# Perceptron down products of a float32 transformer kernel: seven products of block sums per eighth instead of eight block products

## The chip, the cores and the metric

The kernel runs on one NeuronCore of a Trainium2 chip. Its engines work side by side from their own instruction streams and meet at semaphores: TensorE (PE, matmul; its weight loads are shown apart as PEld), VectorE (DVE), ScalarE (ACT), GpSimd (POOL), and SyncE (SP), which issues the loads from the chip's memory. The metric is the device time of one execution, in microseconds (us). A measurement of this kernel can tell a change of about 0.2% (4 us).

## The reference, cut to what matters

The program is three transformer blocks on 512 tokens of width 1024, in float32. The first has a mixture of experts, the other two (layers l = 0 and l = 1 here) end in the perceptron that the change is about:

```
x = x + relu(rms_norm(x, mlp_norm[l]) @ w1[l]) ** 2 @ w2[l]     # x: 512 x 1024, w1: 1024 x 4096, w2: 4096 x 1024
```

After layer 0's perceptron come the projections and the attention of layer 1, after layer 1's the final norm and the output.

## The kernel before

Every engine's instructions are written out by hand in the order in which they run, and semaphores say what waits for what.

**Split products.** A float32 operand a is split as a = hi + lo, where hi is a rounded to the narrower type fp32r and lo = a - hi. A product is three matmuls, hi*hi, hi*lo, lo*hi, added up in a PSUM bank (`split_product`, recorded at L1311). ACT makes each hi (a Copy into an fp32r tile), and a subtraction makes each lo: POOL for weights (`w_lo`, L1023), DVE for activations. Each matmul has 128 rows of contraction and a 128 x 512 result.

**The perceptron.** The 4096 hidden features are done in eighths of 512, in the order up0, up1, down0, up2, down1, ... up7, down6, down7 (`MLP_STEPS`). An up step is four jobs of 24 matmuls (8 blocks of contraction x 3), one for each 128 features; ACT takes the result out of PSUM with Relu and squares it into `hid_hi`, DVE squares it too and subtracts for `hid_lo`. A down step is eight jobs of 12 matmuls (4 blocks x 3): four token tiles t for the first 512 columns of the result, four for the second; DVE adds each job's result to x (`add_to_x`, 128 x 512). So an eighth is 96 + 96 = 192 matmuls.

**PSUM.** Of the eight banks the jobs of the perceptron use two in turn, `psA0` and `psA1`: a job may begin when the result of the job two before it is taken out (semaphores `proj_ready`, `proj_evacuated`). The pairs `psS`, `psT` and `psO` belong to the attentions and are idle in the perceptrons.

**Weights.** Each step's 2 MB of weights comes by one DMA into one of three slots of `ring`. ACT and POOL split them in two halves of 128 x 2048 per step into two pairs of buffers; a half can be split when the half two before it is used up (`then_split`). The last step of layer 0 and both output projections ("ao", "no") end in a norm that is woven in (`norm`, `tail`): per tile of 128 tokens an addition to x, the mean square on ACT and DVE, transposes on PE, and a split of the turned result, whose lo part POOL makes for tiles 0 and 1 and DVE for tiles 2 and 3 (`hT_lo`). The first up job of a layer (`first_hidden`, L1420) takes the first three token tiles in its 384-column matmuls and the fourth in 128-column ones.

Of the kernel before, what the change touches and what calls it, by code (L numbers as in the profile page):

```python
# [6 lines left out]
F32 = mybir.dt.float32  # L7
# [6 lines left out]
P = 128  # L14
# [93 lines left out]
EIGHTHS = 8  # L108
UP_JOBS, DOWN_JOBS = NF // EIGHTHS, 2 * NT

# [13 lines left out]
MLP_JOBS = EIGHTHS * (UP_JOBS + DOWN_JOBS)  # L124

# [60 lines left out]
def split_pieces():  # L186
# [23 lines left out]
    for l, name in enumerate(("ao", "no")):  # L210
# [3 lines left out]
        for kind, e, first in MLP_STEPS:  # L214
            if kind == "up":
                stage(f"up{l}{e}", KD, halves, f"mlp{l}", first, 2)
            else:
                stage(f"down{l}{e}", UP_JOBS, ((0, 512), (512, 1024)), f"mlp{l}", first, NT)
# [10 lines left out]
for _n, _piece in enumerate(SPLIT):  # L229
    SPLIT_AT.setdefault(_piece[0], _n)  # L230
MERGE_AT = {_piece: SPLIT_AT["cp"] + _n for _n, _piece in enumerate(MERGE_ORDER)}
# [94 lines left out]
def build(nc, w, out):  # L326
    ctx = ExitStack()
    with ctx:
# [93 lines left out]
        w_lo = [over(f"w_lo{i}", [P, 2048], "big", 8192 + 2048 * i) for i in range(2)]  # L422
        last_hi, last_lo = [w_lo[0], w_hi[1]], [w_lo[1], w_hi[0]]
        hid_hi = [over(f"hid_hi{i}", [P, UP_JOBS, T], *at) for i, at in enumerate((("tok", 0), ("big", 12288)))]
        hid_lo = [over(f"hid_lo{i}", [P, UP_JOBS, T], *at) for i, at in enumerate((("tok", 2048), ("big", 14336)))]
# [91 lines left out]
        squared = sem("squared")  # L517
        hidden_hi = sem("hidden_hi")
# [205 lines left out]
        S, PR = ([scr[:, i, :] for i in at] for at in ((0, 1), (2, 3, 4)))  # L724

# [87 lines left out]
        slot_of = {n: i % RING for i, n in enumerate(in_ring)}  # L813
# [4 lines left out]
        for name, pieces, _ in plan:  # L818
            if name != "experts":
                total[slot_of[name]] += 16 * len(pieces)  # L820
                arrived_at[name] = total[slot_of[name]]

# [10 lines left out]
        def last_use(name, last):  # L833

            if last == "ax":
                return ax_ready, NT
            if isinstance(last, str):
# [6 lines left out]


# [16 lines left out]
        def raw_piece(c):  # L862

            name, k, c0, c1, _, _ = SPLIT[c]
            words = [pieces[0][1] for n, pieces, _ in plan if n == name][0]
            return slot(name)[:, 0:words].rearrange("p (k n) -> p k n", k=k)[:, :, c0:c1]

        def part(parts, c):

            _, k, c0, c1, _, _ = SPLIT[c]  # L870
            if c < SPLIT_AT["ao0"]:
# [18 lines left out]
        def piece_used(eng, c):  # L890

            if SPLIT_AT["cp"] <= c < SPLIT_AT["ai"]:
# [23 lines left out]
        def _(sp):  # L916
# [75 lines left out]
            for name, pieces, last in plan:  # L992
# [16 lines left out]
                held[s] = last_use(name, last)  # L1009

# [7 lines left out]
        def _(pool):  # L1018
# [82 lines left out]
            def layer(l, out):  # L1101

                split_weight(SPLIT_AT[out + "0"] + 1)
                for c in range(3):
                    then_split(SPLIT_AT[out + "0"] + c)
# [1982 lines left out]
```

## Time and profile before

| | us |
|---|---|
| median of three runs | 2098.33 |
| lowest and highest | 2096.97, 2100.91 |
| the profiled execution | 2099.13 |
| its span, from the first to the last instruction | 2097.3 |

The profiled execution is the one that all rows below come from. It is 0.8 us longer than the median; its span leaves out 1.8 us around the instructions. A row's busy time is the sum of the durations of an engine's instructions; a matmul's end is modelled, so the time from one matmul's start to the next tells its cost, not its duration. "idle before" is the time an engine stood still ahead of an instruction, with what released it.

### The profile page before, as it was taken

To read this page: it belongs to the slowest core of one execution; us is meant where nothing else is said; L and a number is where in the kernel's file an instruction comes from. 1 tells how busy PE (TensorE), PEld (TensorE's weight loads), DVE (VectorE), ACT (ScalarE), POOL (GpSimd) and SP (SyncE) were. 2 spreads that over 40 slices of the span, in tenths; PEclk is the share of its full clock that TensorE was granted. 3 is DMA by queue.
4 is the path that set the end of the run, shared out by engine and by line. 5 is a ranking of instruction groups with operands and counts; after the bars stand their busy time and mean duration, and the time that the engine had idled before them with its cause. 6 is when DMAs were issued, how large, how long until landed. Compare 5 with 4: busy or idle time off the path is not lost.

```text
span 2097.3 us, 27184 instructions
## 1 busy us (share of the span) xinstructions
PE 1911.0 (91%) x10934; PEld 1483.5 (71%) x10934; DVE 748.4 (36%) x1736; ACT 706.8 (34%) x1303; POOL 687.8 (33%) x395
## 2 busy tenths in 40 slices
PE   7999999598885999988999999999799999999998
PEld 6877778432222793457888888888667797888886
DVE  2160343511111525863322222222566623222223
ACT  5123551311111423363423222242267633222322
POOL 2343232011101220154344444443056444444342
PEclk9999999799998899999999999999899999999999
DMA  6232103689998330201223232221500022232311
GB/s 226 81 114 87 41 1 141 260 333 419 420 421 314 112 113 9 80 1 42 81 89 112 81 119 82 83 62 41 121 1 2 2 81 81 80 121 81 121 41 40
DMA packets 82319, 248.44 MB, mean 118 GB/s; under 512 B 12259, under 2 KB 15523, under 8 KB 69904
## 3 DMA queue, kind: packets, MB, share of 16 engines
q1 hardware_dynamic: 75936, 231.54, 30.0%
q0 software_dynamic: 4880, 9.89, 1.3%
q10 hardware_dynamic: 1376, 5.25, 0.6%
q8 instruction: 88, 1.44, 0.3%
q14 instruction: 39, 0.32, 0.1%
HBM read 241.89 MB, written 12.58 MB: 121 GB/s over the span
## 4 chain that ended last, share of the span: by engine, by line
PE 50%; DVE 3%; issue 2%; ACT 1%; POOL 0%; DVEq 0%; ACTq 0%
PE psA L1311 41%; PE psO L1784 2%; PE psT L1821 1%; PE psS L1812 1%; PE psA L1420 1%; PE psO L1371 1%; PE psA L1812 1%; PE psT L1403 1%; DVE scr L3041 1%; ACT big L1853 1%; PE psA L1728 0%; PE psA L1180 0%; DVE scr L2333 0%; DVE nsa_q L2333 0%; PE psO L1774 0%
## 5 line engine op out<-in xcount | busy, mean ns | idle before, releaser
L1023 POOL TENSOR_TENSOR w_lo<-ring,w_hi 128x2048 fp32r<-128x2048 f32 (+2 forms) x43 | 194.9, 4534 | 282.5 <-ACT w_hi L1853 282.5
L2333 DVE TENSOR_TENSOR x<-psA,x 128x512 f32<-128x512 f32 (+1 forms) x176 | 108.7, 618 | 324.6 <-PE psA L1311 320.6
L1853 ACT ACTIVATE w_hi<-ring 128x2048 fp32r<-128x2048 f32 (+2 forms) x65 | 117.6, 1808 | 236.6 <-PE psA L1311 236.6
L1311 PE MATMUL psA<-w_hi,hid_hi 128*128 128x512 f32 x512 | 178.7, 390 | 0.0
L1311 PE MATMUL psA<-w_lo,hid_hi 128*128 128x512 f32 x512 | 178.6, 390 | 0.0
L1311 PE MATMUL psA<-hT_hi,w_hi 128*128 128x512 f32 x504 | 176.8, 390 | 0.0
L1311 PE MATMUL psA<-hT_hi,w_lo 128*128 128x512 f32 x488 | 171.9, 390 | 0.0
L1853 ACT ACTIVATE big<-psA 128x512 f32<-128x512 f32 (+6 forms) x149 | 66.2, 468 | 279.8 <-PE psA L1311 150.1
L2333 DVE TENSOR_TENSOR scr<-scr 128x512 f32<-128x512 f32 (+2 forms) x69 | 62.2, 903 | 275.0 <-ACT hid_hi L1853 274.8
L1311 PE MATMUL psA<-w_hi,hid_lo 128*128 128x512 f32 x384 | 149.6, 390 | 0.0
L1853 ACT ACTIVATE scr<-scr,stat 128x384 f32<-128x384 f32 (+3 forms) x224 | 124.4, 556 | 71.0 <-DVE stat L3041 39.1
L1311 PE MATMUL psA<-hT_lo,w_hi 128*128 128x512 f32 x376 | 146.4, 389 | 0.0
L1023 POOL TENSOR_TENSOR ring_lo<-ring,early_hi 128x1024 fp32r<-128x1024 f32 x36 | 87.1, 2423 | 165.5 <-ACT early_hi L1853 165.5
L1023 POOL TENSOR_TENSOR w_hi<-ring,w_hi 128x2048 fp32r<-128x2048 f32 x18 | 83.2, 4620 | 111.2 <-ACT w_hi L1853 111.2
L1853 ACT ACTIVATE scr<-psA 128x512 f32<-128x512 f32 x64 | 38.2, 597 | 234.5 <-PE psA L1311 218.1
L1023 POOL TENSOR_TENSOR w_lo<-ring,w_lo 128x2048 fp32r<-128x2048 f32 x17 | 78.3, 4606 | 113.8 <-ACT w_lo L1853 113.8
L1156 POOL TENSOR_SCALAR scr<-scr,stat,big 128x128 f32<-128x128 f32 (+3 forms) x128 | 77.0, 612 | 117.2 <-DVE stat L3003 116.9
L1311 PE MATMUL psA<-w_hi,hT_hi 128*128 128x256 f32 (+2 forms) x384 | 108.9, 283 | 5.8 <-DVE tok L2337 2.7
L1311 PEld LDWEIGHTS psA<-w_hi,hid_hi 128*128 128x128 f32 x512 | 96.2, 188 | 20.2 <-DVE scr L2333 0.2
L1311 PEld LDWEIGHTS psA<-w_lo,hid_hi 128*128 128x128 f32 x512 | 96.2, 188 | 19.9
L1311 PEld LDWEIGHTS psA<-hT_hi,w_hi 128*128 128x128 f32 x504 | 94.7, 188 | 19.6
L1311 PE MATMUL psA<-w_lo,hT_hi 128*128 128x256 f32 (+2 forms) x384 | 108.3, 282 | 0.0
(358 smaller groups left out, 4528.1 us busy)
## 6 DMA issues: line engine op xcount, KB each, us to landing
ring<-in_mlp_w SPq DMA_DIRECT2D x32, 2048.0 KB, 8.4
ring<-in_w_in SPq DMA_DIRECT2D x8, 2048.0 KB, 7.9
ring<-in_w_gate_e SPq DMA_DIRECT2D x14, 1024.0 KB, 17.3
ring<-in_w_up_e SPq DMA_DIRECT2D x14, 1024.0 KB, 21.4
ring<-in_w_down_e SPq DMA_DIRECT2D x13, 1024.0 KB, 27.9
big<-in_w_down_e SPq DMA_DIRECT2D x12, 1024.0 KB, 27.5
ring<-in_ab_w_in SPq DMA_DIRECT2D x5, 2048.0 KB, 8.0
scr<-in_w_down_e SPq DMA_DIRECT2D x7, 1024.0 KB, 26.7
```

What stands on the lines that cost most here:

```text
L1023: nc.gpsimd.tensor_tensor(part(w_lo, c), raw_piece(c), part(w_hi, c).bitcast(F32), ALU.subtract)\
L1156: nc.gpsimd.tensor_scalar(at, at, fac[:, n_items + i:n_items + i + 1], gate3[:, it["t"], it["head"], 1 + it["branch"]:2 + it["branch"]], A ...
L1311: ins = pe.matmul(o, a, b, start=(at == 1), stop=(at == 3 * len(terms)))
L1371: ins = pe.matmul(o[HD * half:HD * (half + 1), t * P:(t + 1) * P], v[:, b, 2 * it["hp"] + half, :], pt[half][:, b * P:(b + 1) * P], start= ...
L1403: ins = pe.transpose(psT[k % 2][:, b * P:(b + 1) * P], pair_probs[k % PROBS][:, b * P:(b + 1) * P], ident)
L1420: ins = pe.matmul(o[:, some], a[:, k, 0:P], b[:, k, some], start=(k == 0 and a is wh and b is hT_hi), stop=(k == KD - 1 and a is wl))
L1784: ins = pe.matmul(o[HD * g:HD * (g + 1), at:at + P], v2[:, b, branch, g, 0:HD], pt[g][:, b * P:(b + 1) * P], start=(it["first"] and not br ...
L1812: ins = pe.matmul(o[:, 0:it["n"]], query(4 * it["c"] + it["j"], it["g"])[:, it["t"] * P:(it["t"] + 1) * P], nsa_k[:, it["branch"], it["g"] ...
L1821: ins = pe.transpose(psT[k % 2][:, b * P:(b + 1) * P], probs[k % PROBS][:, b * P:(b + 1) * P], ident)
L1853: return nc.scalar.activation(o, i, f, **kw)
L2333: return nc.vector.tensor_tensor(o, a, b, op)
L3041: nc.vector.tensor_tensor_reduce(out=at, in0=score_bank(i)[:, 0:it["n"]], in1=cmask(it["t"]), scale=-1.0, scalar=3e38, op0=ALU.add, op1=AL ...
```

## The change

In down0 to down6 the product of the hidden block H (512 tokens x 512 features) and the weight block W (512 features x 1024 columns) is done by Strassen's scheme in Winograd's manner. H is cut in four parts a11, a12, a21, a22 (256 tokens x 256 features), W in b11, b12, b21, b22 (256 features x 512 columns). Instead of eight products of parts there are seven, q = 0 to 6, of parts and of sums of parts, and each is added into one, two, three or four quarters of x:

| q | hidden part | weight block | goes to quarters of x | kept in |
|---|---|---|---|---|
| 0 | a12 | b21 | 1 | psA |
| 1 | a11 | b11 | 4 | psS |
| 2 | a12 less a sum | b22 | 1 | psA |
| 3 | a21 + a22 | b12 - b11 | 2 | psT |
| 4 | a11 - a21 | b22 - b12 | 2 | psA |
| 5 | a sum of three | a sum of three | 3 | psO |
| 6 | a22 | b21 less a sum | 1 | psA |

A product q is two token tiles x two blocks of contraction x three = 12 matmuls. The products 0, 2, 4, 6 ("shared") go through `psA` and DVE adds them to x in each down step, in 2, 2, 4 and 2 additions of 128 x 512. The products 1, 3 and 5 ("kept") are added up in the six banks of `psS`, `psT` and `psO` over all seven down steps, and DVE adds them to x once, in 18 additions, during down7. down7 itself stays as it was, except that its weights are split in four pieces.

The work around it changes as follows.

- ACT writes the squares as plain float32 into `raw`. DVE makes four sums of hidden parts (`sum_part`), ACT rounds seven parts (`round_part`) and DVE makes their seven lo parts (`low_part`), all 128 x 512. Two of the parts are rounded after the second up job, two after the fourth, the last three (with the sums they need) at the start of the next up step, while PE does the down step before them or that up step.
- DVE makes four sums of weight blocks in place in the ring (`sum_block`) and the seven lo parts of weight blocks (`low_block`), 128 x 1024 each. POOL no longer touches the weights of down0 to down6.
- All weight pieces of the perceptrons are 128 x 1024 and go through four slots (`w_slot`): piece i can be rounded when piece i - 4 is used up.
- The perceptrons' weights use two slots of the ring; the third holds hidden parts. The slot of a down step's weights is free when the last of its lo parts is made.

The core of the diff (the helpers of DVE and PE; ACT's `round_weight` and `round_part` are a wait and a Copy each):

```
 EIGHTHS = 8
+LAST = EIGHTHS - 1
+PRODUCTS, KEPT, SHARED = 7, (1, 3, 5), (0, 2, 4, 6)
...
+        hidden_parts = [a12, a11, spare, a21, spare, a11, a22]
+        PART_ORDER = (1, 4, 0, 6, 3, 5, 2)
...
+            def down_part(l, e, q):
+
+                pe.wait_ge(down_hi, PRODUCTS * (LAST * l + e) + q + 1)
+                pe.wait_ge(down_lo, PRODUCTS * (LAST * l + e) + q + 1)
+                wh, wl = operand(l, MLP_PIECE_AT["down", e, q])
+                hi, lo = (hid_parts[l, e % 2, q, low] for low in range(2))
+                for t in range(2):
+                    at = slice(t * P, (t + 1) * P)
+                    if q in SHARED:
+                        split_product(job(f"mlp{l}", MLP_FIRST["down", e] + 2 * SHARED.index(q) + t), 512,
+                                      [(hi[:, k, at], lo[:, k, at], wh[:, k, :], wl[:, k, :]) for k in range(2)])
+                        continue
...
+                    for k in range(2):
+                        for a, b in ((hi, wh), (hi, wl), (lo, wh)):
+                            ins = pe.matmul(KEPT_BANK[q][t][:, :], a[:, k, at], b[:, k, :],
+                                            start=(not e and k == 0 and a is hi and b is wh),
+                                            stop=(e == LAST - 1 and k == 1 and a is lo))
...
+            def sum_block(l, e, q):
+
+                n = BLOCK_SUMS.index(q)
+                b11, b12, b21, b22 = (quarter(l, e, k, j) for k in range(2) for j in range(2))
+                if n != 1:
+                    dve.wait_ge(down_lo, PRODUCTS * (LAST * l + e) + (2, None, 4, 6)[n])
...
+                o, a, b = ((b11, b12, b11), (b12, b22, b12), (b11, b22, b11), (b11, b21, b11))[n]
+                tt(o, a, b, ALU.subtract).then_inc(block_sum, 1)
...
             def mlp(l):
                 for kind, e, first in MLP_STEPS:
...
+                    if kind == "up":
+                        if e:
+                            hidden_tail(l, e - 1)
+                            low_block(l, e - 1, 0)
...
+                            low_block(l, e - 1, 1)
+                            sum_block(l, e - 1, 3)
+                            sum_block(l, e - 1, 4)
+                        if e < LAST:
+                            sum_part(l, e, 4)
+                            low_part(l, e, 0)
+                            low_part(l, e, 1)
...
+                            low_block(l, e - 1, 2)
...
+                    elif e < LAST:
+                        low_block(l, e, 3)
+                        add_shared(l, e, 0)
+                        sum_block(l, e, 5)
+                        low_block(l, e, 4)
+                        low_block(l, e, 5)
+                        add_shared(l, e, 2)
+                        sum_block(l, e, 6)
+                        low_block(l, e, 6)
+                        add_shared(l, e, 4)
+                        add_shared(l, e, 6)
```

How this moves instructions is shown at two places. First DVE in a steady down step of layer 0. Before, the hidden block's last square and lo part stand ahead of the eight additions to x, and the next up step follows:

```order
L2333 TENSOR_TENSOR scr<-scr 128x512 [waits hidden_hi]
L2333 TENSOR_TENSOR hid_lo_70<-scr,hid_hi_68 128x512 [waits squared]
L2333 TENSOR_TENSOR x<-psA,x 128x512 [waits proj_ready] x8
L2333 TENSOR_TENSOR scr<-scr 128x512 [waits hidden_hi]
L2333 TENSOR_TENSOR hid_lo_71<-scr,hid_hi_69 128x512 [waits squared]
```

Now the same engine in a down step, from the lo part of product 3's weights (the first row) to the last addition; `ring<-ring` is a sum of weight blocks, `w_slot<-ring,w_slot` the lo part of one:

```order
L2508 TENSOR_TENSOR w_slot_69<-ring,w_slot_69 128x1024 [waits down_hi]
L2508 TENSOR_TENSOR x<-psA,x 128x512 [waits proj_ready] x2
L2508 TENSOR_TENSOR ring<-ring 128x2x512 [waits block_sum,down_lo]
L2508 TENSOR_TENSOR w_slot_71<-ring,w_slot_71 128x1024 [waits down_hi]
L2508 TENSOR_TENSOR w_slot_68<-ring,w_slot_68 128x1024 [waits down_hi]
L2508 TENSOR_TENSOR x<-psA,x 128x512 [waits proj_ready] x2
L2508 TENSOR_TENSOR ring<-ring 128x2x512 [waits block_sum,down_lo]
L2508 TENSOR_TENSOR w_slot_70<-ring,w_slot_70 128x1024 [waits down_hi]
L2508 TENSOR_TENSOR x<-psA,x 128x512 [waits proj_ready]
L2508 TENSOR_TENSOR x<-psA,x 128x512
L2508 TENSOR_TENSOR x<-psA,x 128x512 [waits proj_ready]
L2508 TENSOR_TENSOR x<-psA,x 128x512
```

So the additions that free PE's banks now queue behind weight work on the same engine, and four of them take one bank twice. Second, DVE in down7 of layer 0, where before only eight additions stood: the kept sums (from `psS`, `psT`, `psO`) are put between the first four of them.

```order
L2508 TENSOR_TENSOR x_49<-psA0,x_49 128x512 [waits proj_ready,sum_taken]
L2508 TENSOR_TENSOR x_49<-psS0,x_49 128x512 [waits down_product]
L2508 TENSOR_TENSOR x_49<-psS1,x_49 128x512 [waits down_product]
L2508 TENSOR_TENSOR x_49<-psS0,x_49 128x512 [waits down_product]
L2508 TENSOR_TENSOR x_49<-psA1,x_49 128x512 [waits proj_ready,sum_taken]
L2508 TENSOR_TENSOR x_49<-psS1,x_49 128x512 [waits down_product]
```

## Rows read from the trace of the kernel before

**Rows 1.** The page: busy time of each engine; the chain that ended last.

```profile
PE 1911.0 (91%) x10934; PEld 1483.5 (71%) x10934; DVE 748.4 (36%) x1736; ACT 706.8 (34%) x1303; POOL 687.8 (33%) x395
...
PE psA L1311 41%; PE psO L1784 2%; PE psT L1821 1%; PE psS L1812 1%; PE psA L1420 1%; PE psO L1371 1%; PE psA L1812 1%; PE psT L1403 1%; DVE scr L3041 1%; ACT big L1853 1%; PE psA L1728 0%; PE psA L1180 0%; DVE scr L2333 0%; DVE nsa_q L2333 0%; PE psO L1774 0%
```

**Rows 2.** Stretches: length, busy PE, PEld, DVE, ACT, POOL, granted clock, DMA share, GB/s.

```profile
1060.00:1360.00 300.00, 300.00 (x1325) 248.56 (x1324) 83.85 (x112) 83.90 (x80) 128.99 (x28) 1.00 0.26 92
1780.00:2080.00 300.00, 300.00 (x1326) 248.53 (x1325) 83.36 (x113) 81.06 (x77) 124.39 (x27) 1.00 0.22 78
1072.10:1115.62 43.52, 43.52 (x193) 36.05 (x193) 12.01 (x17) 12.37 (x13) 18.42 (x4) 1.00 0.28 97
```

**Rows 3.** Timeline, PE: matmuls around the start of down1 (start, duration).

```profile
1112.73 0.39 PE L1311 MATMUL psA<-w_hi,hid_hi 128*128 128x512 f32 x1
...
1115.45 0.39 PE L1311 MATMUL psA<-w_hi,hid_hi 128*128 128x512 f32 x1
```

**Rows 4.** Timeline, DVE and POOL in one eighth.

```profile
1072.13 0.69 DVE L2333 TENSOR_TENSOR x<-psA,x 128x512 f32<-128x512 f32 x1
...
1108.78 1.63 DVE L2333 TENSOR_TENSOR scr<-scr 128x512 f32<-128x512 f32 x1 [4.02 <-ACT hid_hi L1853]
...
1115.65 0.69 DVE L2333 TENSOR_TENSOR x<-psA,x 128x512 f32<-128x512 f32 x1
1118.37 0.69 DVE L2333 TENSOR_TENSOR x<-psA,x 128x512 f32<-128x512 f32 x1 [2.03 <-PE psA L1311]
```

```profile
1105.26 4.60 POOL L1023 TENSOR_TENSOR w_lo<-ring,w_hi 128x2048 fp32r<-128x2048 f32 x1 [7.36 <-ACT w_hi L1853]
1116.14 4.60 POOL L1023 TENSOR_TENSOR w_lo<-ring,w_hi 128x2048 fp32r<-128x2048 f32 x1 [6.28 <-ACT w_hi L1853]
```

**Rows 5.** Groups of one form over the span: busy us, mean ns.

```profile
L2333 DVE TENSOR_TENSOR x<-psA,x 128x512 f32<-128x512 f32 x128 | 88.5, 691 | 221.2 <-PE psA L1311 221.0
L2333 DVE TENSOR_TENSOR scr<-scr 128x512 f32<-128x512 f32 x64 | 61.2, 955 | 274.8 <-ACT hid_hi L1853 274.8
L2333 DVE TENSOR_TENSOR hid_lo<-scr,hid_hi 128x512 fp32r<-128x512 f32 x64 | 44.3, 692 | 2.2
```

```profile
L1853 ACT ACTIVATE hid_hi<-scr 128x512 fp32r<-128x512 f32 x64 | 40.4, 632 | 2.1
L1853 ACT ACTIVATE early_hi<-ring 128x1024 fp32r<-128x1024 f32 x36 | 37.9, 1055 | 35.3 <-PE psA L1311 35.3
```

```profile
L1023 POOL TENSOR_TENSOR ring_lo<-ring,early_hi 128x1024 fp32r<-128x1024 f32 x36 | 87.1, 2423 | 165.5 <-ACT early_hi L1853 165.5
```

**Rows 6.** DVE's 128 x 1024 subtractions: one tile (ns min/median/max), then timelines, DVE and POOL.

```profile
L2333 DVE TENSOR_TENSOR second_lo<-hT,second_hi x4: 1216/1219/5546, 702.8 to 706.2; 128x1024 fp32r<-128x1024 f32 x4
```

```profile
702.85 8.95 DVE L2333 TENSOR_TENSOR second_lo<-hT,second_hi 128x1024 fp32r<-128x1024 f32 x4
```

```profile
705.96 4.76 POOL L1023 TENSOR_TENSOR ring_lo<-ring,second_w_hi 128x2048 fp32r<-128x2048 f32 x1 [11.33 <-ACT second_w_hi L1853]
```

**Rows 7.** Timeline, DVE: two instructions in a row on PSUM.

```profile
1371.34 0.69 DVE L2333 TENSOR_TENSOR x<-psA,x 128x512 f32<-128x512 f32 x1
1371.94 0.68 DVE L2333 TENSOR_TENSOR scr<-psA,vec 128x512 f32<-128x512 f32 x1
```

**Rows 8.** The start of layer 0's perceptron: timelines of DVE, then PE.

```profile
1020.14 3.43 DVE L2333 TENSOR_TENSOR hT_lo<-scr,hT_hi 128x512 fp32r<-128x512 f32 x4
```

```profile
1022.62 0.41 PE L1420 MATMUL psA<-hT_hi,w_hi 128*128 128x384 f32 x1 [3.35 <-DVE hT_lo L2333]
```

```profile
1028.42 0.22 PE L1420 MATMUL psA<-hT_hi,w_hi 128*128 128x128 f32 x1
```

**Rows 9.** The end of the kernel: timeline, DVE.

```profile
2079.28 0.69 DVE L2333 TENSOR_TENSOR x<-psA,x 128x512 f32<-128x512 f32 x1 [2.03 <-PE psA L1311]
...
2083.01 0.69 DVE L2333 TENSOR_TENSOR x<-psA,x 128x512 f32<-128x512 f32 x1
```

**Rows 10.** The page's DMA issues: KB each, median us from issue to landing.

```profile
ring<-in_mlp_w SPq DMA_DIRECT2D x32, 2048.0 KB, 8.4
```

More of the change, by code:

```diff
@@ L124 @@
 MLP_JOBS = EIGHTHS * (UP_JOBS + DOWN_JOBS)
+MLP_PIECES = [(kind, e, n) for kind, e, _ in MLP_STEPS
+              for n in range(PRODUCTS if kind == "down" and e < LAST else UP_JOBS)]
+MLP_PIECE_AT = {piece: i for i, piece in enumerate(MLP_PIECES)}
+MLP_FIRST = {(kind, e): first for kind, e, first in MLP_STEPS}
 JOBS, WIDTH = {}, {}
@@ L1009, in _ @@
                 held[s] = last_use(name, last)
+                if name == f"down0{LAST - 1}":
+                    held[spare_slot[0]] = (proj_ready, job("mlp0", MLP_FIRST["down", LAST - 1] + DOWN_JOBS - 1) + 1)
             for t in range(NT):
@@ new lines, in mlp @@
+                    if kind == "up":
+                        for f in range(UP_JOBS):
+                            wh, wl = piece(c + f)
+                            if not (e or f):
+                                first_hidden(job(stage, first), (TAIL["ao"], TAIL["no"])[l], wh, wl)
+                                continue
+                            split_product(job(stage, first + f), T,
+                                          [(wh[:, k, :], wl[:, k, :], hT_hi[:, k, :], hT_lo[:, k, :]) for k in range(KD)])
+                    elif e < LAST:
+                        pe.wait_ge(part_hi, PRODUCTS * (LAST * l + e + 1))
+                        pe.wait_ge(part_lo, PRODUCTS * (LAST * l + e + 1))
+                        for q in range(PRODUCTS):
+                            down_part(l, e, q)
+                    else:
+                        pe.wait_ge(hidden_lo, (l + 1) * UP_JOBS)
+                        pe.wait_ge(hidden_hi, (l + 1) * UP_JOBS)
+                        for half in range(2):
+                            upper, lower = piece(c + 2 * half), piece(c + 2 * half + 1)
@@ new lines, in low_block, with add_shared @@
+            def low_block(l, e, q):
+                dve.wait_ge(down_hi, PRODUCTS * (LAST * l + e) + q + 1)
+                hi, lo = operand(l, MLP_PIECE_AT["down", e, q])
+                tt(lo, blocks_of(l, e)[q], hi.bitcast(F32), ALU.subtract).then_inc(down_lo, 1)
+            def add_shared(l, e, q):
+                for t in range(2):
+                    n = job(f"mlp{l}", MLP_FIRST["down", e] + 2 * SHARED.index(q) + t)
+                    product(dve, n)
+                    for i, j in SHARED_BLOCKS[q]:
+                        xs = x[:, 2 * i + t, 512 * j:512 * (j + 1)]
+                        ins = tt(xs, bank(n)[:, :], xs, ALU.add)
+                    ins.then_inc(proj_evacuated[n % 2], 1)
```

293 lines of the change are left out of this document (232 added, 61 removed).

## The prediction, made before the changed kernel was run

> **What bounds the kernel now.** The page first: PE is busy 91% of the span, DVE 36%, ACT 34%, POOL 33%, and 41% of the chain that ended last is the matmul line L1311 [rows 1]. That is an average over stages, so next the two stretches well inside the perceptrons. In each 300 us of them PE is busy 300.00 us at a granted clock of 1.00, its higher level of 2.4 GHz; DVE has 83 to 84 us, ACT 81 to 84 and POOL 124 to 129 [rows 2]. PE is the bound there, without a gap, and each other engine waits for it: the additions to x stand 2.03 us idle until a product is there [rows 4]. What a matmul costs is read from starts: job 0 of down1 begins at 1112.73 and job 1, twelve matmuls later, at 1115.45 [rows 3], so 2.72 us for 12, 0.2267 us each. The same addition recurs at 1072.13 and 1115.65 [rows 4]: 43.52 us for an eighth of 192 matmuls.
>
> **What it removes.** Down0 to down6 have 84 matmuls instead of 96 (7 x 12 instead of 8 x 12). In two layers that is 2 x 7 x 12 = 168 matmuls fewer, and 168 x 0.2267 = 38.1 us, if PE stays the bound. An eighth then lasts 180 x 0.2267 = 40.8 us. The shape of a matmul does not change, nor does its weight load, and writing six more banks is no more work for PE, so I take the same 0.2267.
>
> The Trainium skill (TensorE: Matmul & The Clock Gate, Wait — 56ns, not 53.3ns?) gives a start-to-start time of columns over 2.4 GHz plus about 2.5 ns, which is an estimate of 215.8 ns for 512 columns; by it the 168 would be worth 36.3 us. The rows show 226.7 for this kernel's split products, so the row goes into the sum.
>
> **What it adds, per eighth.** Durations: a DVE instruction of 128 x 512 takes 0.69 [rows 5], of 128 x 1024 1.22 where nothing blocks it [rows 6]; in a row they follow at 0.60, since the next begins before the last ends [rows 7], and 1.13 by the same 0.09. ACT: 0.63 for 512, 1.06 for 1024; POOL 2.42 for 1024 [rows 5].
> - DVE: 11 sums and lo parts of hidden data and 10 additions at 0.69, 11 sums and lo parts of weights at 1.22: 14.5 + 13.4 = 27.9 us, against 12.0 before [rows 2]. At the pitch in a row it is 12.6 + 12.4 = 25.0.
> - ACT: 8 + 7 at 0.63 and 11 at 1.06: 21.1 us, against 12.4.
> - POOL: four at 2.42, 9.7 us, against 18.4.
>
> All three stay under 40.8, but DVE may be blocked by POOL too. At 1108.78 a DVE instruction with both inputs in SBUF takes 1.63 instead of 0.69 while POOL's subtraction runs from 1105.26 to 1109.86: it ends 0.55 after POOL does. The addition at 1118.37, with one input in PSUM, takes 0.69 in the middle of POOL's next one [rows 4]. And at 702.85 four DVE subtractions of 1024 take 8.95, one of them 5.55, because POOL came at 705.96 and had its turn between the third and the fourth [rows 6]. So I charge DVE all of POOL's time as well: 27.9 + 9.7 = 37.6 of 40.8 us. It fits, with 3.2 to spare.
>
> The Trainium skill (SBUF — State Buffer, Who interferes with whom) has this as an exclusive lock between GpSimd and a DVE instruction with two SBUF inputs, held for the whole instruction by whoever came first. The trace agrees with it. It is the rule that speaks against this change, which puts 22 such instructions into each eighth where there were eight.
>
> **Does the order leave PE waiting?** Room on average is not enough; DVE is one queue, so I work out one down step at full durations. Time 0 is the start of product 0, a product q starts at 2.72 q, and its result is seen 0.20 after it (1115.45 to 1115.65 [rows 3, 4]). ACT: Relu and square of the last up job to 1.5, rounding of the block of product 3 to 2.5. DVE: its lo part to 3.7; two additions 5.1; sum for product 5 6.3; lo parts of 4 and 5 8.8 (ACT has rounded 5 by 7.4); two additions 10.1; sum for 6 11.3, ACT rounds it by 12.4, lo part 13.6; then the four additions of product 4, to 15.0 for the first bank and 16.4 for the second. Product 6 needs its weights and the first bank at 16.3, the second at 17.7. **Slack 1.3 us.** Its first result is seen at 17.9 and added by 18.6; the next up job wants that bank at 19.0, slack 0.4, and only an idle DVE matters for it. In the up step that follows (21.8 us) DVE has 0.9 left over, 8 x 0.69 for the hidden tail, 2.4 behind POOL, and later, held by ACT's rounding of the second block at 13.4, 3 x 1.22 + 3 x 0.69 + 1.22, to about 20.4: 1.4 ahead of the next step. Every up weight is rounded three products (8.2 us) or more ahead of its use and needs 1.06 + 2.42. The ring has two slots: a down step's load can start at 13.6 and takes 8.4 [rows 10], so it is there at 22.0, and its first rounding is due about 26; were it late, PE would want it only at 40.8. So in the steady eighths I cost all that was added at nothing, with DVE's queue as the cover and 1.3 us as its thickness.
>
> **The ends of a layer cost something.**
> - Start: PE already waits 3.35 us for the lo parts of the third tile, and uses the fourth from 1028.42 [rows 8]. The first 1024-wide piece after the norm reaches POOL about 0.9 earlier than the 2048-wide one did, so POOL can have its turn twice between DVE's four subtractions, 4.8 us: the last ends about 1028.4 instead of 1023.6. Cost between 0 and 1.6 a layer (1.6 were PE at its higher clock in this stretch); I take 0.2, since the two times are nearly equal.
> - Down7: its second weight piece is rounded when product 4 is used up, at 13.8, behind other roundings at 14.9, and POOL takes 2 x 2.42 from 13.6: 18.5, due 19.0. Between 0 and 0.6; I take 0.
> - Tail: 18 kept sums and the first four additions go through DVE from 0.9 on. At 0.60 they are done at 14.1, at 0.69 at 16.1; the fifth result is seen at 13.8. So the tail starts 0.3 to 2.3 late. At the kernel's end the delay passes through in full, as the tiles there follow DVE and ACT at 3.73 (2079.28 to 2083.01 [rows 9]) and not PE. I take 0.6 there, nearer the pitch of [rows 7], and 0.3 in layer 0.
>
> Sum: -38.1 + 0.4 + 0.6 + 0.3 = **-36.8 us**, from the profiled 2099.1 to 2062.3. That execution lies 0.8 above the median, so the prediction is **2061.5**, between 2060 with nothing lost at the ends and 2066 with their upper bounds.
>
> **Rivals.**
> 1. *DVE's queue is a little late in every eighth.* The chain up to the second additions of product 4 is 15 us of DVE and ACT with 1.3 of slack; waits that are passed from DVE to ACT and back cost a little each, 0.1 for each of some 13 steps would use it up, and a POOL turn that falls inside it costs 2.4. Beyond that point each microsecond is paid 14 times. A typical overrun of 0.3 to 1.7 costs 4 to 24: 2066 to 2085. For it: the additions that free the banks stand behind weight work. Against: POOL has nothing to do between its last up piece and the first one of the next step, which is released after the last lo part.
> 2. *DVE becomes the bound.* If the 22 instructions with two SBUF inputs cost what the blocked groups show, 955 ns [rows 5] and, by the mean of [rows 6] (three at 1.22, one at 5.55), 2.3 us, an eighth is 11 x 0.955 + 11 x 2.3 + 10 x 0.69 = 42.7 us of DVE, and with the some 5 us in which it must wait for ACT and PE in its order, 47.7. That is 4.2 more than 43.5, 14 times: 58 slower, **2157**. It decides once DVE's eighth passes 43.5. Against: POOL is busy only 9.7 us in an eighth and cannot block for more.
> 3. *The saving is given back*, the products being saved but the wait moved to the layer's ends or to loads: within 4 of 2098. Nothing in the rows has that size; the order shows the 168 matmuls gone, so the change does what it says.
>
> **Chances.** The forecast (2058 to 2066) 0.62; rival 1 0.22 (2066 to 2090); below 2058 0.04; rival 3 0.03; rival 2 or something of its sign 0.09. 2058 to 2084 holds a little over 8 in 10. More than 0.2% faster: 0.88; within 0.2%, 0.03; slower 0.09. 0.2% is about what a measurement of this kernel can tell from no change.
>
> **What would show it.** In the changed profile: PE 168 matmuls fewer and busy about 38 us less; in the perceptrons no idle time of PE and additions of the same kind 40.8 us apart; DVE about 28 us an eighth plus up to 9.7 blocked; PE idle at the first matmul of product 6 or of product 4 would be rival 1, DVE without idle time rival 2. The forecast is wrong if a matmul into the kept banks costs other than 0.2267, or if DVE's 1024-wide instructions exceed 1.22 where POOL is idle.

## The result, and the profile after

The kernel after takes **2063.93 us** (median of four, 2060.58 to 2065.47), the kernel before 2098.26 beside it (2096.97 to 2100.91): 34.3 us faster by the medians. The ratio put on record for these runs is 0.9827, 95% interval 0.9815 to 0.9839; it is not the quotient of the two medians, which is 0.9836, and by it the gain is 36.3 us. The forecast was 2061.5, range 2058 to 2084. Direction and mechanism came true; the median is 2.4 us above it, which is looked into below. The profiled execution of after is the 2060.58 one, the fastest of its four; its span is 2058.8.

The page's busy times, the counterpart of [rows 1]: PE has 168 matmuls fewer and 38.2 us less, DVE 254 us more, ACT 111 more, POOL 120 less. A busy time counts a moment in which two instructions of an engine overlap once; it is not the sum of their durations, as it was called ahead of the prediction.

```profile
PE 1872.8 (91%) x10766; PEld 1451.1 (70%) x10766; DVE 1002.3 (49%) x1996; ACT 818.0 (40%) x1507; POOL 568.3 (28%) x403
```

Stretches inside the perceptrons and one eighth, as [rows 2] (length, busy PE, PEld, DVE, ACT, POOL, granted clock, DMA share, GB/s):

```profile
1040.00:1340.00 300.00, 300.00 (x1325) 248.41 (x1324) 211.18 (x244) 144.13 (x185) 72.32 (x30) 1.00 0.29 102
...
1066.00:1106.80 40.80, 40.80 (x182) 33.78 (x181) 28.49 (x33) 20.24 (x26) 9.66 (x4) 1.00 0.28 103
```

PE has still no gap, and an eighth is 40.80 us, 2.72 less. DVE went from 12.0 to 28.5 us of it, against 27.9 worked out; ACT to 20.2 (21.1), POOL to 9.7 (9.7). For DVE the two don't count the same thing, which is taken up below. One down step on PE, then the same stretch on DVE, ACT and POOL:

```profile
1107.11 2.88 PE L1417 MATMUL psA<-w_slot,hid_part 128*128 128x512 f32 x12
1109.83 2.88 PE L1575 MATMUL psS<-w_slot,hid_part 128*128 128x512 f32 x12
...
1120.71 2.88 PE L1575 MATMUL psO<-w_slot,hid_part 128*128 128x512 f32 x12
1123.43 2.88 PE L1417 MATMUL psA<-w_slot,hid_part 128*128 128x512 f32 x12
```

```profile
1116.72 1.21 DVE L2508 TENSOR_TENSOR ring<-ring 128x1024 f32<-128x1024 f32 x1
1119.06 1.23 DVE L2508 TENSOR_TENSOR w_slot<-ring,w_slot 128x1024 fp32r<-128x1024 f32 x1 [1.13 <-ACT w_slot L1988]
1120.20 2.48 DVE L2508 TENSOR_TENSOR x<-psA,x 128x512 f32<-128x512 f32 x4
...
1126.95 0.89 DVE L2508 TENSOR_TENSOR scr<-scr 128x512 f32<-128x512 f32 x1
1127.77 2.88 DVE L2508 TENSOR_TENSOR hid_part<-scr,hid_part 128x512 fp32r<-128x512 f32 x1
```

```profile
1120.12 7.18 POOL L1126 TENSOR_TENSOR w_slot<-ring,w_slot 128x1024 fp32r<-128x1024 f32 x3 [30.82 <-ACT w_slot L1988]
1127.62 2.48 POOL L1126 TENSOR_TENSOR w_slot<-ring,w_slot 128x1024 fp32r<-128x1024 f32 x1 [0.32 <-ACT w_slot L1988]
```

Products follow at 2.72, in the kept banks (L1575) too. The lo part for product 6 ends 13.2 after the step's start (worked out: 13.6), the additions of product 4 run from 13.1 to 15.6 (16.4). POOL's three pieces for the next up step start at 1120.12, in the last 0.2 us of the last lo part (1119.06 to 1120.29), and lie beside the four additions, which have an input in PSUM; the first DVE instruction after them with two SBUF inputs is lightly touched (0.89), the next (2.88) waits one POOL turn.

**Where the 34 us came from.** Four marks that all traces have: the first product of layer 0's perceptron, the first product after its norm, the first product of layer 1's perceptron, the end of the span. The marks of the kernel before are [rows 8] and the ones below, then those of after:

```profile
1381.20 0.36 PE L1311 MATMUL psA<-w_hi,hT_hi 128*128 128x256 f32 x1 [0.51 <-DVE scr L2333]
1736.01 0.41 PE L1420 MATMUL psA<-hT_hi,w_lo 128*128 128x384 f32 x1 [3.35 <-DVE hT_lo L2333]
```

```profile
1019.24 0.66 PE L1526 MATMUL psA<-hT_hi,w_slot 128*128 128x384 f32 x1 [3.34 <-DVE hT_lo L2508]
1359.67 0.48 PE L1417 MATMUL psA<-w_slot,hT_hi 128*128 128x256 f32 x2 [0.51 <-DVE scr L2508]
1715.94 0.41 PE L1526 MATMUL psA<-hT_hi,w_slot 128*128 128x384 f32 x1 [3.35 <-DVE hT_lo L2508]
```

The same marks in every trace of this study, in us (perceptron 0 with its norm; the code between the perceptrons, which is the same in all; perceptron 1 with the end):

| trace | start | perceptron 0 | between | perceptron 1 |
|---|---|---|---|---|
| before | 1022.62 | 358.58 | 354.81 | 361.29 |
| before, second trace | 1021.09 | 359.05 | 354.60 | 361.36 |
| after | 1019.24 | 340.43 | 356.27 | 342.86 |
| after, second trace | 1024.01 | 340.59 | 356.45 | 342.85 |
| 12 matmuls a step put back | 1022.40 | 359.63 | 356.37 | 362.80 |
| 2 DVE additions from SBUF, late | 1020.50 | 382.22 | 357.57 | 385.71 |
| 2 DVE additions from SBUF, early | 1022.38 | 341.06 | 357.59 | 344.37 |
| 2 DVE additions from PSUM | 1022.59 | 340.41 | 356.09 | 342.81 |
| 4 DVE additions from PSUM | 1021.16 | 345.63 | 354.67 | 347.84 |
| nothing kept over the eighths | 1019.89 | 391.31 | 356.29 | 393.91 |
| kept sums left out | 1019.07 | 340.09 | 358.88 | 343.16 |
| up products of 21 matmuls | 1024.14 | 320.81 | 357.36 | 324.09 |
| up products of 18 matmuls | 1025.01 | 316.47 | 356.07 | 319.35 |

The two perceptrons became 18.3 and 18.5 us shorter (means of two traces each), **36.8 together, the forecast's sum**. The first trace of before enters perceptron 0 at the higher clock and the other three at the lower one; those three alone give 18.5 and 37.0. The start differs by up to 6 us between traces with the same code ahead of it; that is the kernel's run-to-run spread. And the middle is 1.5 to 1.9 us longer in after, by either trace. The trace says why. Here is the whole middle of before and of after (length, busy PE with its matmuls, granted clock, DMA):

```profile
1381.20:1736.01 354.81, 320.40 (x2849) 0.97 0.15 43
```

```profile
1359.67:1715.94 356.27, 321.72 (x2849) 0.96 0.14 37
```

The waits of PE there are the same ones, of the same length; the same 2849 matmuls take 1.3 us longer. Twenty us from 40 us behind the mark show one place, before's first trace, then after's first (the second trace of each gives the same clock and count):

```profile
1421.20:1441.20 20.00, 17.26 (x154) 1.00 0.31 107
```

```profile
1399.67:1419.67 20.00, 17.25 (x134) 0.91 0.30 106
```

PE is equally busy but gets 20 matmuls fewer done at 0.91. Of the eleven traces of changed kernels in the table two were granted 1.00 in these 20 us. One (4 additions from PSUM) has a middle of 354.67, as before's. The other (up products of 21 matmuls) has 357.36; its clock falls in the 20 us behind them instead:

```profile
1404.95:1424.95 20.00, 18.09 (x169) 0.91 0.01 2
```

So what counts is the whole middle. In the trace's record of the clock the lower level holds there for 23.9 us in before's two traces and with 4 additions from PSUM (354.60 to 354.81 long), for 27.3 us in after's two and in two more (356.07 to 356.45), and for 28.6 to 32.2 us in the other six (356.29 to 358.88). The same instructions in the same order can thus be granted another clock. When they come doesn't settle it by itself: with 12 matmuls a step put back the middle starts at 1382.03, within 2 us of before's, and is 356.37 long. What decides it is not known.

### The profile page after: what moved, and what is told of

Read it like the earlier page. It is cut to its first block, busy times and chain, and to the rows that moved or that the text cites. A ratio compares the mean times of both kernels' runs of the same rounds, so it can differ in the third digit from the quotient of the medians.

```text
span 2058.8 us, 27648 instructions
## 1 busy us (share of the span) xinstructions
PE 1872.8 (91%) x10766; PEld 1451.1 (70%) x10766; DVE 1002.3 (49%) x1996; ACT 818.0 (40%) x1507; POOL 568.3 (28%) x403
## 4 chain that ended last, share of the span: by engine, by line
PE 48%; DVE 4%; issue 2%; ACT 2%; POOL 0%; DVEq 0%; ACTq 0%
PE psA L1417 33%; PE psO L1575 2%; PE psT L1575 2%; PE psS L1575 2%; PE psO L1918 2%; PE psT L1955 1%; DVE x L2508 1%; PE psS L1946 1%; PE psA L1526 1%; PE psO L1477 1%; PE psT L1509 1%; PE psA L1946 1%; DVE scr L3332 1%; ACT big L1988 1%; PE psA L1862 0%
## 5 line engine op out<-in xcount | busy, mean ns | idle before, releaser
L1126 POOL TENSOR_TENSOR w_slot<-ring,w_slot 128x1024 fp32r<-128x1024 f32 (+2 forms) x80 | 208.5, 2620 | 542.1 <-ACT w_slot L1988 541.9
L1417 PE MATMUL psA<-hT_hi,w_slot 128*128 128x512 f32 x992 | 307.8, 389 | 0.0
L1988 ACT ACTIVATE w_slot<-ring 128x1024 fp32r<-128x1024 f32 (+2 forms) x178 | 192.0, 1088 | 176.9 <-PE psA L1417 76.9
L1417 PEld LDWEIGHTS psA<-hT_hi,w_slot 128*128 128x128 f32 x992 | 186.2, 188 | 38.6
L1417 PE MATMUL psA<-hT_lo,w_slot 128*128 128x512 f32 x496 | 192.9, 389 | 0.0
L2508 DVE TENSOR_TENSOR w_slot<-ring,w_slot 128x1024 fp32r<-128x1024 f32 x98 | 119.9, 1224 | 116.0 <-ACT w_slot L1988 116.0
L1417 PE MATMUL psA<-w_slot,hid_part 128*128 128x512 f32 x672 | 161.4, 389 | 0.0
L1988 ACT ACTIVATE scr<-scr,stat 128x384 f32<-128x384 f32 (+3 forms) x224 | 124.3, 556 | 71.1 <-DVE stat L3332 39.4
L1417 PEld LDWEIGHTS psA<-w_slot,hid_part 128*128 128x128 f32 x672 | 126.1, 188 | 26.2
L1417 PEld LDWEIGHTS psA<-hT_lo,w_slot 128*128 128x128 f32 x496 | 93.1, 188 | 19.3
L1714 PE MATMUL psS<-ring,big 128*64 128x512 f32 x224 | 83.3, 683 | 19.4 <-issue 18.5
L2508 DVE TENSOR_TENSOR hid_part<-scr,hid_part 128x512 fp32r<-128x512 f32 x98 | 98.3, 1027 | 4.9 <-ACT hid_part L1988 3.7
## 6 DMA issues: line engine op xcount, KB each, us to landing
ring<-in_w_down_e SPq DMA_DIRECT2D x13, 1024.0 KB, 28.5
```

What stands on the lines that cost most here:

```text
L1126: nc.gpsimd.tensor_tensor(part(w_lo, c), raw_piece(c), part(w_hi, c).bitcast(F32), ALU.subtract)\
L1417: ins = pe.matmul(o, a, b, start=(at == 1), stop=(at == 3 * len(terms)))
L1714: ins = pe.matmul(psS[p][at:at + ROWS, :].rearrange("p (h n) -> p h n", h=2), xT[:, p, k, at:at + ROWS], gu[(2 * b + half) % UNITS][:, k], ...
L1988: return nc.scalar.activation(o, i, f, **kw)
L2508: return nc.vector.tensor_tensor(o, a, b, op)
```

## The experiments

**The changed kernel again, and the kernel before again.** No edit.

> The changed kernel once more, nothing edited, to see how much of its time differs from run to run before the perceptrons. Theory T (PE alone bounds both kernels in the perceptrons; 168 matmuls fewer are worth 38.1 us, the ends take 0.8 back): ratio 0.981 to 0.984, and the stretch from the first up product of layer 0 to the first product after the norm again 340.4 us within 0.3, whatever the start of that stretch is. Rival L (DVE's queue is a little late now and then): that stretch differs by more than 1 us between profiled executions, with idle time of PE in front of the down products.

Measured: 2064.09 us (five runs) beside 2099.16 of before (fifteen): ratio 0.9827, 0.9812 to 0.9842, 35.1 us. The stretch of perceptron 0 is 340.59, within 0.2 of the first trace, with a start 4.8 us later. PE is busy 300.00 of 300 us again. Rival 1's occasional lateness would show here; it doesn't.

> The kernel before, nothing edited, for its trace. Theory T: its stretch from the first up product of layer 0 to the first product after the norm is again 358.6 us within 0.3, and the start of that stretch may lie several us from the 1022.6 of the first trace, as the code ahead of it is the same in both kernels.

Measured: 359.05, 0.47 from the first trace where at most 0.3 was expected, and a start at 1021.09. The clock at the mark differs, which probably is the 0.47: the first matmul of 384 columns takes 0.66 here and 0.41 in [rows 8], that is, this one starts at the lower of the two levels, as both traces of after do.

**The added work without the saving.** Product 5 is multiplied twice.

```
-                    for k in range(2):
-                        for a, b in ((hi, wh), (hi, wl), (lo, wh)):
...
+                    turns = 2 if q == 5 else 1
+                    for turn in range(turns):
+                        for k in range(2):
+                            for a, b in ((hi, wh), (hi, wl), (lo, wh)):
...
```

> The changed kernel with product 5 of every down step multiplied twice into its kept banks (its result is then counted twice), so that a down step has 96 matmuls again and all the added work of DVE, ACT and POOL stays. Theory T: 2 x 7 x 12 x 0.2267 = 38.1 us slower than the changed kernel, so 1 us slower than the kernel before within its noise (ratio to it 0.999 to 1.002), an eighth of 43.52 us. Rival L: some of the added work already costs time in the changed kernel, so putting matmuls back hides it: less than 36 us slower than the changed kernel.

Measured: 2103.46 us, 39.4 above the changed kernel and 4.3 above before (ratio 1.002, 1.001 to 1.003). Expected 38.1 and 1. By the stretches, which leave the rest of the program out: 359.63 and 362.80, 19.1 and 19.9 more than after, 39.0 in all. PE's gain is given back in full by 168 matmuls, so the added DVE and ACT work cost nothing in the steady part (PE is busy 300.00 of 300 us there too). Against before's mean the two stretches are 0.8 and 1.5 longer, the price of the ends; perceptron 1 starts at the lower clock here (0.66 against 0.41 for its first matmul), which is part of the 1.5.

**How thick is DVE's slack?** Additions whose sums go to idle words, in each of the 14 down steps. First two with both inputs in SBUF, ahead of the additions of product 4:

```
                         low_block(l, e, 6)
+                        for o in (idle[l], S[0], S[1], stat[:, 0:2, :].rearrange("p a n -> p (a n)"))[0:2]:
+                            tt(o, prm("final")[:, 0:512], prm("final")[:, 512:1024], ALU.add)
                         add_shared(l, e, 4)
```

> The changed kernel with two additions of 128 x 512 from SBUF on DVE ahead of the two additions of product 4 in every down step (their sums go to idle words), 1.2 us in the chain that frees the first bank. Theory T: that bank is free at about 14.4 us from the start of the step in the trace and is wanted at 16.3, a slack of 1.9, so nothing changes (within 1.5 us of the changed kernel). The forecast's own slack of 1.3 gives nothing either. Rival L (no slack): 14 x 1.2 = 17 us slower.

Measured: 2149.34 us, **85 slower** where nothing was expected. The two instructions do not take 1.2 us there. DVE, POOL and PE of that kernel:

```profile
1126.91 1.23 DVE L2508 TENSOR_TENSOR w_slot<-ring,w_slot 128x1024 fp32r<-128x1024 f32 x1 [1.13 <-ACT w_slot L1988]
1128.05 2.89 DVE L2508 TENSOR_TENSOR ring<-par 128x512 f32<-128x512 f32 x1
1130.87 2.85 DVE L2508 TENSOR_TENSOR scr<-par 128x512 f32<-128x512 f32 x1
1133.64 2.47 DVE L2508 TENSOR_TENSOR x<-psA,x 128x512 f32<-128x512 f32 x4
```

```profile
1127.97 7.96 POOL L1126 TENSOR_TENSOR w_slot<-ring,w_slot 128x1024 fp32r<-128x1024 f32 x3 [30.58 <-ACT w_slot L1988]
```

```profile
1128.56 2.88 PE L1575 MATMUL psO<-w_slot,hid_part 128*128 128x512 f32 x12
...
1135.06 5.46 PE L1417 MATMUL psA<-w_slot,hid_part 128*128 128x512 f32 x12 [3.62 <-DVE x L2508]
1140.32 0.63 PE L1417 MATMUL psA<-hT_hi,w_slot 128*128 128x512 f32 x1
```

Each waits about 2.2 us while one of POOL's pieces runs, so 5.6 us stand in the chain in place of 1.2. Product 6 was due 2.72 behind product 5, at 1131.28, and starts at 1135.06, 3.8 late. After the wait PE gets its lower clock: the twelve matmuls from 1135.06 to 1140.32 take 5.26 instead of 2.72.

```profile
1135.06:1140.32 5.26, 5.26 (x13) 4.10 (x13) 1.74 (x3) 0.00 (x0) 0.87 (x1) 0.50 0.03 10
```

So a step costs 3.8 + 2.5, less what falls elsewhere: measured (382.22 - 340.5) / 7 = 6.0, fourteen times 83. Two rivals were left: that the chain has no slack for any DVE work, or that the place in the order matters and not where the inputs lie. Three runs tell them apart.

The same two instructions, ahead of the block sum for product 6, where POOL is idle:

> The same two DVE additions of 128 x 512 from SBUF in every down step, but ahead of the block sum for product 6, where POOL has nothing to do, instead of ahead of the additions of product 4, where POOL's next three pieces run. Theory T2 (what cost 85 us in the first such run was POOL's turn between DVE instructions of two SBUF inputs, 5.74 us instead of 1.3, plus the clock that PE lost by waiting): here they cost their own 1.2, inside the slack of 1.9, so no change, within 2 us of the changed kernel. Rival L (the chain has no slack for DVE work at all): 17 us slower or more.

Measured: 2066.69 us, 2.6 above the changed kernel, a little over the 2 expected; its runs spread over 2.9. The stretches are 0.5 and 1.5 longer, the second with its start at the lower clock, and the middle, which the edit doesn't touch, is 1.2 longer. The instructions take 0.68 each, product 6 never waits, and in 300 us PE waits once, 0.4 us, for a POOL piece.

```profile
1119.84 0.68 DVE L2508 TENSOR_TENSOR ring<-par 128x512 f32<-128x512 f32 x1
1120.43 0.68 DVE L2508 TENSOR_TENSOR scr<-par 128x512 f32<-128x512 f32 x1
```

At the late place again, but with one input from PSUM, two and then four of them:

```
                     product(dve, n)
+                    idle = ring[:, spare_slot[l], 3584:4096]
+                    for o in (idle, S[0], S[1], stat[:, 0:2, :].rearrange("p a n -> p (a n)"))[0:2 if q == 4 and t == 0 else 0]:
+                        tt(o, bank(n)[:, :], prm("final")[:, 0:512], ALU.add)
```

> The changed kernel with two more DVE additions of 128 x 512 in every down step, right ahead of the additions of product 4, at the place where two SBUF additions cost 85 us; these take one input from the PSUM bank of product 4. Theory T2: an input in PSUM does not wait for POOL, so they take 0.60 each, 1.2 in all, inside the slack of 1.9: no change, within 2 us. Rival L: 17 us slower or more; were the place and not the port what matters, 85.

Measured: 2063.11 us, no change; stretches 340.41 and 342.81. The place alone is harmless; two inputs in SBUF beside POOL's pieces are not.

> As the run before, with four such additions, 2.4 us. Theory T2: the first bank is free at 16.8 from the start of the step and wanted at 16.3, so PE waits 0.5 to 0.6 in each of 14 steps: 7 to 8 us slower than the changed kernel, if so short a wait doesn't lower the granted clock; if it does, as the wait of 3.6 did at 2.6 us a step, up to 14 x 3.1 = 43. With the forecast's slack of 1.3 instead of 1.9 it were 14 x 1.1 = 15. No slack: 34 or more.

Measured: 2071.20 us, 7.1 above the changed kernel by the medians, 10.1 by the two stretches (the middle is 1.7 shorter here); expected 7 to 8 if the clock holds. It does (1.00 in the windows). Product 6 starts 0.60 late in this step:

```profile
1122.97 0.68 DVE L2508 TENSOR_TENSOR ring<-psA,par 128x512 f32<-128x512 f32 x1
1123.57 1.28 DVE L2508 TENSOR_TENSOR scr<-psA,par 128x512 f32<-128x512 f32 x2
1124.77 0.68 DVE L2508 TENSOR_TENSOR stat<-psA,par 128x512 f32<-128x512 f32 x1
1125.36 2.47 DVE L2508 TENSOR_TENSOR x<-psA,x 128x512 f32<-128x512 f32 x4
```

```profile
1123.47 2.88 PE L1575 MATMUL psO<-w_slot,hid_part 128*128 128x512 f32 x12
1126.79 2.97 PE L1417 MATMUL psA<-w_slot,hid_part 128*128 128x512 f32 x12 [0.43 <-DVE x L2508]
```

2.4 us inserted, 0.60 late: **the slack is 1.8 us**, where the forecast had 1.3.

**Are the kept results needed?** Products 1, 3 and 5 start their banks anew in each step and DVE adds them there:

```
-                                            start=(not e and k == 0 and a is hi and b is wh),
+                                            start=(k == 0 and a is hi and b is wh),
...
                         add_shared(l, e, 6)
+                        for what in kept:
+                            add_kept(l, e, *what)
```

> The changed kernel with nothing kept over the eighths: products 1, 3 and 5 start their banks anew in every down step, and DVE adds them to x behind the additions of product 6, 18 more additions of one PSUM input a step, 10.8 us; none is left for the end of a layer. Theory T (DVE is far from bound in the changed kernel, but not by that much): DVE's eighth becomes 28.5 + 10.8 = 39.3 us plus what POOL's turns and its own order add; in the changed kernel it idles some 12 of 40.8 us, of which some 5 is order. An eighth of 42 to 47 us, so 17 to 90 us slower than the changed kernel, with the clock lowered on top where PE waits. Rival K (keeping the three results is not needed for the gain): within 3 us of the changed kernel.

Measured: 2166.07 us, 102 slower than the changed kernel and 67 slower than before (ratio 1.0327, 1.0309 to 1.0345), above the 17 to 90 expected. The reason given was wrong too: DVE is not full. In 300 us it is busy 227 (84 in the kernel before [rows 2]).

```profile
1040.00:1340.00 300.00, 271.05 (x1152) 221.82 (x1150) 227.15 (x307) 127.49 (x166) 62.34 (x26) 0.95 0.26 92
```

```profile
1134.91 4.87 DVE L2508 TENSOR_TENSOR x<-psS,x 128x512 f32<-128x512 f32 x8
1139.70 2.47 DVE L2508 TENSOR_TENSOR x<-psT,x 128x512 f32<-128x512 f32 x4
1142.09 3.67 DVE L2508 TENSOR_TENSOR x<-psO,x 128x512 f32<-128x512 f32 x6
1145.68 0.68 DVE L2508 TENSOR_TENSOR scr<-scr 128x512 f32<-128x512 f32 x1
```

```profile
1150.06 0.76 PE L1417 MATMUL psA<-hT_hi,w_slot 128*128 128x512 f32 x1 [5.04 <-ACT scr L1988]
```

The 18 additions, 10.8 us, stand in DVE's queue ahead of the hidden tail; ACT rounds the hidden parts only behind it, and has the Relu that frees the next up product's bank behind those roundings. PE waits 5.04 us for that Relu in each step and then runs at the lower clock: (391.31 - 340.5) / 7 = 7.3 a step, 102 in all. DVE has idle time elsewhere in the step (227 of 300 us busy), but in this place the additions make a chain through two queues. So the 102 us are the price of this placing; whether the 18 additions, spread over the step, would cost less was not tried.

**The kept sums at the layer's end.** The 18 additions left out, with the waits on them.

```
-                        kept = [(q, t, i, j) for q in KEPT for i, j in KEPT_BLOCKS[q] for t in range(2)]
+                        kept = []
```

> The changed kernel without the 18 additions of the kept results to x at the end of each layer (products 1, 3 and 5 then never reach x). Theory T: their cost is what they delay the fifth addition of the last down step by, 0.53 us at the kernel's end by the trace, and about 0.3 in layer 0: the stretch from the first up product of layer 0 to the first product after the norm becomes 340.2 instead of 340.5, that from the first up product of layer 1 to the end 342.3 instead of 342.85, the time of the run the same within what it can tell. Rival: the additions cost up to 2.3 us each time, as the upper bound of the forecast has it: stretches shorter by 2 us.

Measured: 2063.92 us, the same. The stretch of perceptron 0 is 340.09, 0.4 shorter than 340.5 (0.3 expected). Perceptron 1's, 343.16, is not shorter, where 342.3 was expected, but starts at the lower clock (0.66). The tail itself is read from the fifth addition against PE's last matmul:

```profile
2043.18 0.69 DVE L2505 TENSOR_TENSOR x<-psA,x 128x512 f32<-128x512 f32 x1 [2.03 <-PE psA L1417]
```

```profile
2050.92 0.39 PE L1417 MATMUL psA<-w_slot,hid_lo 128*128 128x512 f32 x1
```

and in the changed kernel, where the fifth addition has no idle time ahead of it:

```profile
2038.91 1.89 DVE L2508 TENSOR_TENSOR x<-psO,x 128x512 f32<-128x512 f32 x3
2040.71 0.68 DVE L2508 TENSOR_TENSOR x<-psA,x 128x512 f32<-128x512 f32 x1
```

```profile
2047.91 0.39 PE L1417 MATMUL psA<-w_slot,hid_lo 128*128 128x512 f32 x1
```

7.74 us ahead of PE's last matmul without the sums, 7.20 with them: they delay the tail by 0.54.

**How far does PE stay the bound?** The last one, then the last two, of the eight input blocks are left out of every up product but a layer's first.

```
-                                          [(wh[:, k, :], wl[:, k, :], hT_hi[:, k, :], hT_lo[:, k, :]) for k in range(KD)])
+                                          [(wh[:, k, :], wl[:, k, :], hT_hi[:, k, :], hT_lo[:, k, :]) for k in range(KD - 1)])
```

> The changed kernel with the last of the 8 input blocks left out of every up product but the first of each layer, 21 matmuls instead of 24, to see how far PE stays the bound: 2 x (9 + 7 x 12) = 186 matmuls fewer, 38.1 us an eighth. Theory T: the hidden data's lo parts end 2.5 us before the down step in the changed kernel's trace, and follow an up product that now also ends 1.4 earlier, so all 186 come out as time: 186 x 0.2267 = 42 us faster than the changed kernel (40 to 43). Rival D (DVE's 28.5 us plus POOL's 9.7 plus order are all used up): less than 25 us faster.

Measured: 2027.39 us, 36.7 faster than the changed kernel, 38.5 by the stretches, of 42.2 that the 186 matmuls are worth; 40 to 43 was expected. PE is busy 269.49 of 270 us. So PE still bounds, and about a tenth of the gain is missing. Part of it is the clock: perceptron 1 starts at the lower level (0.66 for its first matmul) and gains 0.9 less than perceptron 0, and the middle is 1.0 longer. The rest was not traced.

> As the run before, with the last two input blocks left out, 18 matmuls in an up product: 372 fewer, 35.4 us an eighth if PE were still the bound, 84 us faster than the changed kernel. Theory T: the hidden data's lo parts would end about 0.2 us after the down step is due, and the ring, the rounding and POOL's turns come closer, so PE waits some tenths to 2 us in each of 14 steps: 55 to 84 us faster, less what the clock loses. Rival D: hardly faster than the run with 21.

Measured: 2017.63 us, 46.5 faster, 47.5 by the stretches, below the 55 to 84 expected: of the second 42 us only 9 to 10 arrive. PE waits for ACT's Relu, which frees its bank, twice an eighth (14.0 us in 270):

```profile
1102.91 1.63 PE L1417 MATMUL psA<-w_slot,hid_part 128*128 128x512 f32 x6 [1.72 <-ACT scr L1988]
1105.06 1.66 PE L1417 MATMUL psA<-w_slot,hid_part 128*128 128x512 f32 x6 [0.52 <-ACT scr L1988]
```

The changed kernel thus stands some 3 us an eighth ahead of its next bound, the chain from the up products through ACT and DVE to the down step. DVE is busy 206 of 270 us in this run: again the order, not the sum. At the first of the two, ACT had itself stood idle for 3.89 us, with the Relu queued behind a rounding whose sum DVE had not made.

## Why the prediction was right

- **What it removes.** 168 x 0.2267 = 38.1 us. An eighth is 40.80, PE's busy time in the two perceptrons fell by 37.6 from the first trace of before to the first of after and by 38.0 between the second traces, and putting the matmuls back cost 39.0 by the stretches. The page's 38.2 for the whole program agrees by chance: between the second traces it is 31.1, as the part ahead of the perceptrons differs. Right, also that a kept bank costs PE nothing.
- **What it adds.** The 27.9 is a sum of durations, the 28.5 counts overlaps once, so they are not to be compared. In one eighth the durations of DVE's 32 instructions sum to 30.2, against 27.9 with no POOL turn and 37.6 with all of them. All of POOL's time was charged to DVE; only one turn of four is paid (the 2.88 instead of 0.69), and 0.2 ahead of it (the 0.89). The cover held.
- **The order.** Slack 1.3 from the hand-made timetable, 1.8 measured: lo parts and sums in a row follow at 1.14 and additions at 0.60, and the timetable had charged the full 1.22 and 0.69. The error lay on the safe side.
- **Rival 1** was the one to watch. Its price beyond the threshold was put at 14 us for each microsecond; that holds for short waits (7 to 10 us at 0.60 late), but a wait of 3.6 cost another 2.2 in clock, so 85 where 14 x 3.8 = 53 would have been said. Its argument against was that POOL has nothing to do between its last up piece and the next step's first, which is released after the last lo part. The first half is what the trace shows (30.82 us idle). The second is not: POOL waits for ACT's rounding, which ACT does right behind that for product 6, and starts at 1120.12, before the last lo part ends at 1120.29. That lo part escapes a POOL turn because it is issued 1.06 us ahead of POOL, and not because anything holds POOL back until it is done. This margin, thinner than the 1.8, was not seen.
- **Rival 2.** The mean of 2.3 us for a blocked 1024-wide DVE instruction does not recur: 49 of them take 1224 ns on average in 300 us of the changed kernel. DVE did not become the bound; not even with 10.8 us more (227 of 300 busy).

```profile
L2508 DVE TENSOR_TENSOR w_slot<-ring,w_slot 128x1024 fp32r<-128x1024 f32 x49 | 60.0, 1224 | 58.0 <-ACT w_slot L1988 58.0
...
L2508 DVE TENSOR_TENSOR hid_part<-scr,hid_part 128x512 fp32r<-128x512 f32 x47 | 46.0, 1001 | 1.5 <-ACT hid_part L1988 0.9
```

- **Start of a layer.** Forecast: POOL comes twice between DVE's four subtractions, cost 0.2. It comes once, and they take 5.59 instead of [rows 8]'s 3.43; PE does not wait for the fourth tile, so the cost is 0. A mis-sized term of 0.4 in all: 0.2 a layer was forecast, and nothing is paid.

```profile
1016.77 5.59 DVE L2508 TENSOR_TENSOR hT_lo<-scr,hT_hi 128x512 fp32r<-128x512 f32 x4
```

```profile
1018.96 5.64 POOL L1126 TENSOR_TENSOR w_slot<-ring,w_slot 128x1024 fp32r<-128x1024 f32 x2 [1.12 <-ACT w_slot L1988]
```

- **Tail.** 0.6 and 0.3 forecast, 0.54 and 0.4 measured. Term by term the sum is then 38.1 - 0.9 = 37.2; that the stretches give 36.8 to the tenth is partly luck.
- **What failed.** The sum stopped at the perceptrons' edges: "the profiled time less 36.8" takes the rest of the program as fixed. It is not. The code between the perceptrons runs 1.7 us longer, with the clock granted otherwise there, which leaves 35.1 of 36.8; the two comparisons have 34.3 and 35.1 by their medians, and 36.3 by their ratio of 0.9827, each with 2.5 to 3 us to either side, so they can't tell these apart. What makes the clock fall in that stretch stays open.

By the start-to-start time in the Trainium skill (TensorE: Matmul & The Clock Gate, Wait — 56ns, not 53.3ns?) the matmuls' worth is an estimate of 36.3 us. The eighths side with the row, 2.72 us for twelve. The Trainium skill (SBUF — State Buffer, Who interferes with whom) says that a DVE instruction with at most one SBUF input, outside DVE's 2-port modes, does not contend with GpSimd. The two runs at one and the same place, 1.2 us for two additions with an input in PSUM and 5.6 for two with none, agree.

## What to carry to other kernels

Where PE has no gap, matmuls taken away come out as time at their pitch, and an engine that is idle 70% of the time there, as DVE was, can pay for it with sums of blocks. Results to which every step only adds can be left in PSUM over the steps: adding them each time, all in one place of the queue, cost 102 us, more than the change brings. Judge the added work by the chain in each queue and not by busy time, and put DVE work with two SBUF inputs where POOL is idle: the same two instructions a step cost 3 us or 85, depending on what POOL does beside them. After such a change look at the parts of the program that it did not touch, as their clock may be another (here 1.7 us).

## What the runs showed of the hardware that was not expected

- A short wait of PE (0.4 to 0.7 us a step) left the granted clock at 1.00; one of 3.62 us was followed by twelve matmuls at 0.50, 5.26 us instead of 2.72. A wait's price was 1.6 times its length (6.0 a step for 3.8 late), and 7.3 for 5.04.
- POOL's pieces and DVE instructions with two SBUF inputs took turns one by one: two DVE additions of 0.68 each became 2.89 and 2.85, each behind one POOL piece of 2.4 us.
- The same code, with PE equally busy, was granted 0.91 in one kernel and 1.00 in another for 20 us, the same in both traces of each. Over the thirteen traces its 2849 matmuls ran at the lower level for 23.9 to 32.2 us, and the stretch was 354.60 to 358.88 long, longer with more time at that level in the main.
- A matmul's time has a part that does not go with its columns: 0.2267 us for 512 and 0.12 for 256 columns (before's trace, from 1699.77 to 1706.73, 58 matmuls in 6.96 us) at the higher level leave 13 ns beside the columns.
